# A projection whose first weight group is loaded in two halves between the first token blocks, with its products from the second block's transposes on

## The reference

```python
def rmsnorm(x, g):
    return x * lax.rsqrt(jnp.mean(x * x, axis=-1, keepdims=True) + EPS) * g

hn = rmsnorm(h_res, norm1_g)
proj = hn @ w_in                      # 1024 x 1024 times 1024 x 3072
qa, ka, va, qb, kb, vb = jnp.split(proj, splits, axis=-1)
qa = partial_rope(rmsnorm(qa, da_qk_norm_g[0]), cos, sin)
ka = partial_rope(rmsnorm(ka, da_qk_norm_g[1]), cos, sin)
oa = diff_attention(qa, ka, va, ...)
ob = stick_breaking_attention(qb, kb, vb)
h_res = h_res + concat(oa, ob) @ w_out
h_res = h_res + peer(rmsnorm(h_res, norm2_g), ...)
```

## Time and profile before

| | |
|---|---|
| median of 3 timed runs | 3304.91 us (3301.92 to 3309.66) |
| span of the profiled execution | 3312.1 us |
| PE busy | 3164.1 us, 96% of the span |
| DVE, POOL, ACT busy | 2201.4, 1682.8, 1220.7 us |
| mean granted TensorE clock | 0.984 of full speed |

### The profile page before, as it was taken

How to read it: one execution, slowest core, us unless ns; L and a number is a source line. 1 busy time by engine, 2 the same in 40 slices (tenths; PEclk the granted TensorE clock), 3 DMA queues, 4 the chain that set the end, 5 groups by cost and what they waited for, 6 DMA issues and landing times.

```text
span 3312.1 us, 44104 instructions
## 1 busy us (share of the span) xinstructions
PE 3164.1 (96%) x17090; PEld 2858.3 (86%) x17090; DVE 2201.4 (66%) x3558; ACT 1220.7 (37%) x1899; POOL 1682.8 (51%) x845
## 2 busy tenths in 40 slices
PE   7999879889999999999999999998999999999997
PEld 5887878778899999999999999996888888888886
DVE  3512888534476777888888887764776666675655
ACT  3222557421122236656566556651222222121110
POOL 2510000112125565555655565656878787768783
PEclk9999999999999999999999999998999999999999
DMA  4174533221125776767777766998887887878784
GB/s 141 59 249 122 129 67 86 100 101 45 52 75 194 238 219 227 251 239 246 242 248 243 245 231 236 309 342 313 305 316 289 290 301 285 291 258 295 275 303 161
DMA packets 254387, 713.66 MB, mean 215 GB/s; under 512 B 21776, under 2 KB 79888, under 8 KB 247568
## 3 DMA queue, kind: packets, MB, share of 16 engines
q1 hardware_dynamic: 180496, 443.00, 39.3%
q0 software_dynamic: 73728, 268.47, 23.3%
HBM read 577.18 MB, written 134.22 MB: 215 GB/s over the span
## 4 chain that ended last, share of the span: by engine, by line
PE 52%; DMA 11%; DVE 7%; POOL 6%; issue 3%; ACT 2%; SPq 0%; DVEq 0%; ACTq 0%; POOLq 0%
PE banks L2259 21%; PE banks L1445 19%; DMA found<-in_u,pick_u 6%; PE banks L831 5%; PE banks L1458 3%; DMA v_raw<-in_v 3%; PE banks L810 2%; DVE found L1361 2%; POOL side_lo L2135 2%; DMA gate_in<-gate_d 2%; POOL found L2107 1%; POOL u_lo L1094 1%; DVE col_gate L1149 1%; DVE row_hot L1149 1%; PE banks L839 1%
## 5 line engine op out<-in xcount | busy, mean ns | idle before, releaser
L1361 DVE SCALAR_TENSOR_TENSOR found<-found,x_first 128x1024 f32<-128x1024 f32 x237 | 413.0, 1754 | 227.7 <-DMA found<-in_u,pick_u 226.6
L1094 POOL TENSOR_TENSOR u_lo<-u_raw,u_hi 128x1024 fp32r<-128x1024 f32 x127 | 358.0, 2819 | 354.8 <-ACT u_hi L1023 354.5
L1445 PE MATMUL banks<-side_hi,u_hi 128*128 128x384 f32 x2048 | 529.7, 339 | 0.0
L1445 PE MATMUL banks<-side_lo,u_hi 128*128 128x384 f32 x2048 | 520.9, 335 | 0.0
L1445 PE MATMUL banks<-side_hi,u_lo 128*128 128x384 f32 x2048 | 520.7, 335 | 0.0
L2259 PE MATMUL banks<-side_hi,act_hi 128*128 128x512 f32 x1488 | 460.0, 390 | 11.7 <-POOL act_lo L2139 6.6
L2259 PE MATMUL banks<-side_hi,act_lo 128*128 128x512 f32 x1488 | 459.0, 390 | 0.0
L2259 PE MATMUL banks<-side_lo,act_hi 128*128 128x512 f32 x1488 | 459.0, 390 | 0.0
L1103 POOL DMA_INDIRECT found<-in_u,pick_u x237 | 343.5, 1449 | 190.3 <-DVE found L1361 152.0
L2078 ACT ACTIVATE side_hi<-v_raw 128x2048 fp32r<-128x2048 f32 x62 | 119.0, 1919 | 794.9 <-DMA v_raw<-in_v 727.9
L2164 DVE TENSOR_TENSOR acc<-acc,banks 128x1024 f32<-128x1024 f32 x192 | 234.0, 1219 | 242.6 <-PE banks L2259 230.5
(11 more groups left out here) (243 smaller groups left out, 5495.7 us busy)
## 6 DMA issues: line engine op xcount, KB each, us to landing
u_raw<-in_uT SPq DMA_DIRECT2D x128, 512.0 KB
v_raw<-in_v SPq DMA_DIRECT2D x63, 1024.0 KB
hid_d<-hid SPq DMA_DIRECT2D x128, 384.0 KB
gate_d<-stage SPq DMA_DIRECT2D x48, 1024.0 KB, 8.7
act_in<-hid_d SPq DMA_DIRECT2D x63, 768.0 KB, 4.3
gate_in<-gate_d SPq DMA_DIRECT2D x31, 1536.0 KB
w_raw<-in_w_in SPq DMA_DIRECT2D x6, 2048.0 KB, 8.8
k_hi<-k_hi_d SPq DMA_DIRECT2D x32, 256.0 KB, 7.8
```

The source lines that it names most:

```text
L1094: pool.tensor_tensor(u_lo[s % 2][:, :, :], u_raw[:, :, :], u_hi[s % 2][:, :, :].bitcast(F), ALU.subtract).then_inc(u_lo_ok, 1)
L1361: dve.scalar_tensor_tensor(out=found[:, g], in0=found[:, g], scalar=1.0, in1=x_first[:, g], op0=ALU.mult, op1=ALU.mult, accum_out=pick_act ...
L1445: mm = pe.matmul(hid_ps[:, s % 2, half, 0:W], w[s % 2][:, ch], x[:, ch, GB * P + half * W:GB * P + (half + 1) * W], start=n == 0, stop=n = ...
```

## The change

The separate block for the constants goes; its two transfers become the third (`ident`) and the ninth (`iota`) of `project`. The first weight group is loaded in two halves of 4 chunks, the first ahead of token block 1 and the second behind it. The tables for the heads' norm and rotation move behind block 3. ACT splits the first half right behind the squares of block 0, the second behind `take_block(0)`; DVE now writes the `w_lo` parts 0 and 1 of that group, POOL the parts 2 and 3, each behind the -1/2 power of a token block. PE's list takes one item behind each block's transposes from the second block on, and ACT and DVE handle the item of two blocks ago in each round. The constant -1/2 is written once for the whole program (`neg_half`, 128x8; `neg_heads` for the heads), so that `attend` and the routing no longer write their own.

```diff
+            def load_w_half(half):
+                s = slice(4 * half, 4 * half + 4)
+                sp.dma_start(w_raw[:, s], w_d[4 * half * P:4 * (half + 1) * P, 0:HALF]
+                             .rearrange("(c p) n -> p c n", p=P)).then_inc(w_in if half else w_first_in, 16)
+
             def load_w(g):
-                if g:
-                    sp.wait_ge(w_lo_ok, 4 * g)
+                if g == 1:
+                    sp.wait_ge(w_first_lo, 2)
+                sp.wait_ge(w_lo_ok, 4 * g - 2)
                 sp.dma_start(w_raw[:, :, :], w_d[:, g * HALF:(g + 1) * HALF]
                              .rearrange("(c p) n -> p c n", p=P)).then_inc(w_in, 16)
...
             load_x(0)
             sp.dma_start(gain[:, :], norm_g_d.unsqueeze(0).to_broadcast([P, D])).then_inc(small_in, 16)
-            sp.dma_start(qk_gain[:, :, :], qk_g_d.unsqueeze(0).to_broadcast([P, 2, HD])).then_inc(small_in, 16)
-            sp.dma_start(cos[:, :, :], cos_d.rearrange("(b p) r -> p b r", p=P)).then_inc(small_in, 16)
-            sp.dma_start(sin[:, :, :], sin_d.rearrange("(b p) r -> p b r", p=P)).then_inc(small_in, 16)
-            for tb in range(1, 4):
-                load_x(tb)
-            load_w(0)
+            sp.dma_start(ident[:, :], ident_d).then_inc(small_in, 16)
+            load_w_half(0)
+            load_x(1)
+            load_w_half(1)
+            load_x(2)
+            load_x(3)
+            sp.dma_start(iota[:, :], iota_d).then_inc(later_in, 16)
+            sp.dma_start(qk_gain[:, :, :], qk_g_d.unsqueeze(0).to_broadcast([P, 2, HD])).then_inc(later_in, 16)
+            sp.dma_start(cos[:, :, :], cos_d.rearrange("(b p) r -> p b r", p=P)).then_inc(later_in, 16)
...
                 pool.tensor_tensor(rstd[:, tb:tb + 1], ss[:, tb:tb + 1], neg_half[:, 0:1],
                                    ALU.pow).then_inc(rstd_ok, 1)
-                if tb in (3, 4):
-                    split_low(0, 2 * (tb - 3))
+                if tb < 2:
+                    split_low(0, 2 + tb)
             for g in range(G):
...
         def _(act):
             def split_high(g, part):
                 s = slice(2 * part, 2 * part + 2)
-                act.wait_ge(w_in, 16 * (g + 1))
+                if g == 0 and part < 2:
+                    act.wait_ge(w_first_in, 16)
+                else:
+                    act.wait_ge(w_in, 16 * (g + 1))
                 if g >= 2:
...
+
+            def keep_item(g, k):
+                n = ITEMS * g + k
+                act.wait_ge(pr_ok, n + 1)
+                act.activation(qk[:, g, k], pr_ps[:, n % 4], ACT.Copy)
+                if n >= 2:
+                    act.wait_ge(qss_ok, n - 1)
+                act.activation(sq[:, n % 2], pr_ps[:, n % 4], ACT.Square).then_inc(copied, 1)
+
+            squares(0)
+            split_high(0, 0)
...
+            squares(1)
+            take_block(0)
+            split_high(0, 2)
+            split_high(0, 3)
+            for tb in range(2, TB + 1):
                 if tb < TB:
-                    act.wait_ge(x_in[tb % 4], 16 * (tb // 4 + 1))
-                    if tb:
-                        act.wait_ge(ss_ok, tb)
-                    act.activation(spare[:, :, :].rearrange("p a b -> p (a b)"), x[:, tb % 4], ACT.Square,
-                                   accum_out=ss[:, tb:tb + 1]).then_inc(ss_ok, 1)
-                if tb >= 1:
-                    take_block(tb - 1)
-                if tb in (3, 4):
-                    for part in range(2):
-                        split_high(0, 2 * (tb - 3) + part)
+                    squares(tb)
+                take_block(tb - 1)
+                keep_item(0, tb - 2)
             stored = 0
             for g in range(G):
                 for k in range(ITEMS):
                     n = ITEMS * g + k
                     if g < 2:
-                        act.wait_ge(pr_ok, n + 1)
-                        act.activation(qk[:, g, k], pr_ps[:, n % 4], ACT.Copy)
-                        if n >= 2:
-                            act.wait_ge(qss_ok, n - 1)
-                        act.activation(sq[:, n % 2], pr_ps[:, n % 4], ACT.Square).then_inc(copied, 1)
+                        if n >= ITEMS - 1:
+                            keep_item(g, k)
                     else:
                         slot = out_slot(stored)
                         act.wait_ge(pr_ok, n + 1)
@@ -284,22 +312,38 @@
                 dve.tensor_scalar(ss[:, tb:tb + 1], ss[:, tb:tb + 1], 1.0 / D, EPS, ALU.mult,
                                   ALU.add).then_inc(var_ok, 1)
 
-            dve.wait_ge(small_in, 64)
+            def scale(tb):
+                dve.wait_ge(rstd_ok, tb + 1)
+                dve.scalar_tensor_tensor(out=x[:, tb % 4], in0=x[:, tb % 4], scalar=rstd[:, tb:tb + 1],
+                                         in1=gain[:, :], op0=ALU.mult, op1=ALU.mult).then_inc(xs_ok, 1)
+
+            def first_low(part):
+                s = slice(2 * part, 2 * part + 2)
+                dve.wait_ge(w_hi_ok, part + 1)
...
+
             mean_square(0)
-            for tb in range(TB + 1):
+            dve.wait_ge(small_in, 32)
+            scale(0)
+            first_low(0)
+            mean_square(1)
+            scale(1)
+            low(0)
+            first_low(1)
+            for tb in range(2, TB + 1):
                 if tb < TB:
-                    dve.wait_ge(rstd_ok, tb + 1)
-                    dve.scalar_tensor_tensor(out=x[:, tb % 4], in0=x[:, tb % 4], scalar=rstd[:, tb:tb + 1],
-                                             in1=gain[:, :], op0=ALU.mult, op1=ALU.mult).then_inc(xs_ok, 1)
-                if tb + 1 < TB:
-                    mean_square(tb + 1)
-                if tb >= 1:
-                    low(tb - 1)
-                if tb in (4, 5):
-                    part = 2 * (tb - 4) + 1
-                    dve.wait_ge(w_hi_ok, part + 1)
-                    dve.tensor_tensor(w_lo[:, 0, 2 * part:2 * part + 2], w_raw[:, 2 * part:2 * part + 2],
-                                      w_hi[:, 0, 2 * part:2 * part + 2].bitcast(F), ALU.subtract).then_inc(w_lo_ok, 1)
+                    mean_square(tb)
+                    scale(tb)
+                low(tb - 1)
+                if tb >= 3:
+                    sum_squares(tb - 3)
+            dve.wait_ge(later_in, 128)
...
-                                      ALU.add).then_inc(qss_ok, 1)
+                for k in range(ITEMS - 2 if g == 0 else 0, ITEMS):
+                    sum_squares(ITEMS * g + k)
...
                 for m, (l, r) in enumerate(passes):
+                    if n == 0 and m % 6 == 0:
+                        pe.wait_ge(w_first_lo if m < 12 else w_lo_ok, m // 6 % 2 + 1)
                     last = pe.matmul(pr_ps[:, n % 4], l, r, start=m == 0, stop=m == len(passes) - 1)
...
+            pe.wait_ge(small_in, 32)
             for tb in range(TB):
                 turn_x(tb)
-                if tb == 4:
-                    pe.wait_ge(w_lo_ok, 4)
-                if tb >= 4:
-                    pe.wait_ge(lo_ok, tb - 3)
-                    item(0, tb - 4)
+                if tb >= 1:
+                    pe.wait_ge(lo_ok, tb)
+                    item(0, tb - 1)
             for g in range(G):
                 if g:
-                    pe.wait_ge(w_lo_ok, 4 * (g + 1))
-                for k in range(4 if g == 0 else 0, ITEMS):
+                    pe.wait_ge(w_lo_ok, 4 * g + 2)
+                for k in range(ITEMS - 1 if g == 0 else 0, ITEMS):
                     if g == 0:
                         pe.wait_ge(lo_ok, k + 1)
                     item(g, k)
```

More of the change, by code:

```diff
@@ L34, with project @@
 EPS = 1e-6
[L37 to L38 removed]
+def project(nc, a_hi, a_lo, ident, iota, neg_half, ident_d, iota_d, cos_d, sin_d, x_d, norm_g_d, w_d, qk_g_d,
+            q_hi_d, q_lo_d, k_hi_d, k_lo_d, v_d, mask_raw, mask, unit, lam, sub_g, mask_da_d, mask_sb_d, lam_d, sub_g_d, first_pair, pair_in):
     G = 6
@@ L322, in _ @@
             for g in range(2):
-                for k in range(ITEMS):
-                    n = ITEMS * g + k
-                    dve.wait_ge(copied, n + 1)
-                    dve.tensor_reduce(qk_ss[:, g, k], sq[:, n % 2].rearrange("p (h d) -> p h d", d=HD), AX.X,
-                                      ALU.add).then_inc(qss_ok, 1)
+                for k in range(ITEMS - 2 if g == 0 else 0, ITEMS):
+                    sum_squares(ITEMS * g + k)
                 dve.wait_ge(qss_ok, ITEMS * (g + 1))
@@ L515, in __init__ @@
         self.rstd = small("rstd3", [P, TB])
-        self.neg_half = small("neg_half3", [P, 1])
         self.total = small("total", [P, 2, PEER_HEADS])
@@ L1479, in load_pair, with attend @@
             sp.dma_start(k_lo[here, part].bitcast(F), k_lo_d[n][rows]).then_inc(loaded, 16)
-def attend(nc, ident, mask, unit, lam, sub_g, mix_hi, mix_lo, q_hi_d, q_lo_d, k_hi_d, k_lo_d,
+def attend(nc, ident, neg_half, mask, unit, lam, sub_g, mix_hi, mix_lo, q_hi_d, q_lo_d, k_hi_d, k_lo_d,
```

(11 more changed lines are left out.)

46 lines of the change are left out of this document (26 added, 20 removed).

## The result

The change made the kernel **slower by 1.1%**: a median of 3342.36 us (3338.07 to 3344.91, four runs) against 3306.47 us (3301.92 to 3309.66, four runs), a ratio of 1.0109 with the interval 1.0095 to 1.0124. The prediction had 3304.4 us with 3310.0 as its upper end. So 36 us are to be explained. The part of the kernel that the change touches is not where they come from.

The account below looks back on a forecast made before the run. PE, busy for 96% of the span, was taken as the bound. The 12.0 us earlier start, less 2.8 of transposes, 6.2 idle and 2.5 slow clock, left 0.5 us gained: median 3304.4 us, range 3299.4 to 3310.

Parts of the forecast that it names:

- Costed at nothing: Tables and masks behind block 3, two memsets, and the constants of attend and routing: no time charged.
- What is later moves with it: Everything behind the start of group 1 shifts with that start, if its own margins hold; group 1 was at 83.04 us.
- rivals: Part of the gain stays, 3301.9 us (0.20); whole gain stays, 3295.7 us (0.04); start comes late, 3310.1 us (0.10).
- The first product: Start of the projection: PE's first product at 22.4 us, 12.0 earlier than before.
- POOL wins the race: At block 1's scaling, POOL's part starts 0.06 us ahead of DVE, whose scaling takes 3.42 us instead of 1.28.
- Group 0: Projection's first group: six blocks' transposes among its items instead of three, 51.4 us instead of 48.68, ending at 73.8.
- The wait at group 1: PE idle for 6.2 us from 73.8 until POOL's four w_lo parts are ready at 80.0 us.
- The clock behind it: After the idle time ahead of group 1, PE's clock falls and its products lose 2.5 us.
- not below 2.4, since the idle time here is the longer one: Lower bound on the slow clock's cost at group 1, unless the clock doesn't fall.
- The sum: Start of group 1: 82.5 us against 83.04, so the kernel becomes 0.5 us faster.
- the earlier start: First product 12.0 us earlier, spent on 2.8 us of transposes, 6.2 of idle time and 2.5 of slow clock.

Follow-up runs that it names:

- e5_after_same_distance: The changed kernel with neg_half allocated ahead of side_hi, so all operand distances are as before the change; 3301.46 us, ratio 0.9990.
- e6_power_first: e5_after_same_distance with POOL's power of block 1 ahead of both parts of the second half; 3297.73 us, ratio 0.9975.
- e7_split_early: e6_power_first with ACT splitting group 1 within the last two rounds of the token blocks; 3288.85 us, ratio 0.9943.
- e3_all_32b: The kernel before with an unused 32-byte tile ahead of side_hi, moving every tile and changing no distance; 3306.68 us, ratio 0.9997.
- m1_offsets: Small kernel without the layer: 26 series of 48 products, weights, moving operand or both moved; 226.7 ns a product at the old distance, 233.3 at 32 bytes more.
- m2_offsets: Small kernel like m1_offsets with other distances and both operands moved by different amounts; 48 products take 11.11 us at 16 bytes, 10.89 at 256.

## Why the prediction was wrong

**The step that failed** is the one sentence "Costed at nothing: the tables and masks behind block 3 (needed 40 us later), the two memsets, and the constants of `attend` and routing ...". The instructions do cost next to nothing: `e5_after_same_distance` has them all and is no slower than before. But the constant has a tile, the tile of 32 bytes stands ahead of all later ones, and that changed the distance between the two operands of 6912 products: a term put at nothing that cost 38 us by the spans of this kernel and `e5_after_same_distance`, 41 us by their medians. With it failed "What is later moves with it": it holds only if a product takes in the changed kernel the 0.227 us that it took before, and there it takes 0.233. None of the rivals had this, and the range ended 32 us below the result.

**The other steps, by their own numbers.**
- *The first product*, 22.4: it is 23.04. ACT's first parts start at 10.00 us by the landing of the first half, where 8.8 had been taken; the rest follows, with a scaling of 3.36 us for 3.42. The trace bears out that POOL wins the race.
- *Group 0*, 51.4 us: from 23.04 us, and with the idle time of 5.93 us taken from 80.70, it is 51.73 us. That is luck in part: its 192 products at 6.6 ns more make 1.3 us of it, and in `e5_after_same_distance`, at the old pace, group 0 takes 79.67 - 6.1 - 23.1 = 50.5 us, 0.9 less than predicted. This and the first product, 0.7 late there, nearly cancel, so that group 1 starts at 79.67 against the predicted 80.0.
- *The wait at group 1*, 6.2 us: 5.93, and 6.1 in `e5_after_same_distance`.
- *The clock behind it*, 2.5 us: too large, with 1.7 by the row of the changed kernel and 2.1 by `e6_power_first` and `e7_split_early`. The bound "not below 2.4, since the idle time here is the longer one" failed: idle times of 5.63 us in the earlier trace rows, 5.93 here and 6.09 in `e6_power_first` cost 2.5, 1.7 and 2.1 us, so the length of the idle time doesn't set the price by itself.
- *The sum*, -0.5 us: `e5_after_same_distance` has 0.9990 (0.9978 to 1.0002), a change of -0.2% to nothing, and its last product of the projection in the form `w_lo,side_hi` starts at 306.3 us, before at 307.5. The order of the work is worth about a microsecond there.

**Where the 12 us of the earlier start had gone.** The prediction put 8.7 of them on the idle time and the clock at group 1; with the split in time, 9.3 us come back at the end of the projection. The power ahead of POOL's parts gives something on top of the 12 us, 6.3 us at the first product and 5.5 at the end of the projection. Together they end the projection 306.3 - 291.4 = 14.9 us earlier than in `e5_after_same_distance` (last start of the form `w_lo,side_hi`), and the medians are 3301.46 - 3288.85 = 12.6 us apart.

**What stays open.** Why a wrong distance costs time was not shown. That the load of the next weights gets in the way of the moving operand of the present product would fit a rule on their distance; but no run separates the two reads in time. Nor is it shown why a remainder of 64 bytes costs 2.5 ns, 16 bytes 4.8, and 32, 192 and 224 bytes 6.6. In the whole layer only shifts of 0, 32, 64 and 512 bytes were tried.

## What to carry to other kernels

When a stage that a change doesn't touch gets slower without idle time and at the full clock, compare the counts in a stretch of equal length, and then the addresses of the operands. In a kernel whose tiles are all multiples of 256 bytes the remainder of the distance is 0 until somebody puts a small tile between two operands. Put small tiles ahead of both operands' tiles (`e3_all_32b`, `e5_after_same_distance`) or behind them all, or fill them up to 256 bytes; the last is drawn from the small kernels, and in the layer only 512 bytes were tried. And before a change is given up, separate its order of work from its layout: here the order was sound, and with two further edits it is 0.6% faster than before, while the layout alone cost 1.1 to 1.5%.

## What the runs showed of the hardware

- The pace of products of 512 columns (fp32r, new weights for each) hangs on the distance from the start of the weights to that of the moving operand within a partition, by its remainder in 256 bytes. It is 226.7 ns at 0; 231.5 ns at 16; 229.2 ns at 64; and 233.1 to 233.3 ns at 32, 192 and 224, 2.9% more (`m1_offsets`, `m2_offsets`). Neither operand's own place matters in the series that moved both alike, nor in `e3_all_32b`. The Trainium skill says in the section named above that PE never waits for anyone, and that only the ports shared by DVE and GpSimd cause contention. No run here shows another engine slowing PE; but the pace changes with PE working alone (`m1_offsets`), so that rule doesn't account for all that these products take.
- The slower pace is listed as busy time at a granted clock of 1.00. In the weighing a product in it is listed 6 ns longer, 396 ns for 390, and the count of a stretch falls from 1678 to 1630.
- The experts' products of 384 columns are hit less, if at all: their median duration went from 334 to 336 ns, and their stage took 1265.3 us in the changed kernel and 1274.8 to 1280.1 in the three others with a wrong distance, against 1266.7 to 1273.0 at the old one. The small kernels have no series of 384 columns at this stage's remainders of 224 and 192.
